# Rounded parts in the projections of the state-space stage: three one-pass products in place of one float32 product

## The reference, cut to what matters

```
[cq | ckv | kr | z | xBC | dt | mq | g] = x @ w_in
branch A: latent attention      (cq, ckv, kr)
branch B: xBC -> causal conv (4 taps) -> SiLU -> x, B, C in 4 groups
          dt = softplus(dt_raw + bias); decays exp(cum_i - cum_j)
          y  = ((C B^T) * decay * dt) x  +  C S exp(cum)  +  d_skip x
          S  = S exp(last) + (dt exp(last - cum) B)^T x      (also for the 8 sample states)
          y  = y * silu(z), RMS norm per group
branch M: cross-attention into 256 memory tokens
m  = sig(gA)(oA WoA) + sig(gB)(oB WoB) + sig(gM)(oM WoM);  x1 = LN(alpha x + m w_out)
y  = LN(alpha x1 + relu(x1 w_up + b_up)^2 w_down + b_down)
```

## Time and profile before

| | us |
|---|---|
| median of three runs | 1787.76 |
| the profiled execution | 1788.35 |
| its span, first to last instruction | 1786.7 |
| PE busy | 1712.9 (96%) |
| DVE, ACT, POOL busy | 734.7, 379.3, 370.1 |
| one group of the state-space stage (178.2 to 287.7) | 109.5 |

### The profile page before, as it was taken

One profiled execution on the slowest core, in us unless ns is written; L12 is line 12 of the kernel. 1 busy time (PEld: TensorE's weight loads), 2 busy tenths in 40 slices (PEclk: granted clock), 3 DMA queues, 4 the chain that ended last, 5 costly groups with the idle time before them and its releaser, 6 DMA issues.

```text
span 1786.7 us, 25145 instructions
## 1 busy us (share of the span) xinstructions
PE 1712.9 (96%) x10132; PEld 1416.8 (79%) x10132; DVE 734.7 (41%) x1284; ACT 379.3 (21%) x758; POOL 370.1 (21%) x330
## 2 busy tenths in 40 slices
PE   8999999999999999999899999999996999999995
PEld 6767667677777877787677777778895999999995
DVE  5565667665341121111222212311157871157345
ACT  2151332514312121111011111100124111111122
POOL 0040221402210000000233210000034433434332
PEclk9999999999999999999999999999999999999998
DMA  5324224252253222221777775432221222222221
GB/s 211 116 77 142 89 78 148 77 174 66 85 192 110 65 61 70 71 71 42 236 232 247 239 256 186 156 106 71 72 95 36 83 89 89 84 94 83 89 78 50
DMA packets 70405, 206.18 MB, mean 115 GB/s; under 512 B 10161, under 2 KB 26802, under 8 KB 65682
## 3 DMA queue, kind: packets, MB, share of 16 engines
q1 hardware_dynamic: 50384, 151.67, 26.3%
q10 hardware_dynamic: 13762, 31.93, 5.2%
q0 software_dynamic: 6144, 20.98, 4.0%
HBM read 189.68 MB, written 14.86 MB: 114 GB/s over the span
## 4 chain that ended last, share of the span: by engine, by line
PE 90%; DVE 5%; DMA 2%; ACT 1%; issue 1%; SPq 1%; POOL 0%; POOLq 0%; ACTq 0%; DVEq 0%
PE acc L1638 37%; PE acc L1678 23%; PE acc L1939 6%; PE acc L1905 3%; PE bank L1849 2%; PE acc L1887 2%; PE acc L2042 1%; PE bank L1954 1%; PE bank L1973 1%; PE bank L1955 1%; PE bank L1809 1%; PE bank L2056 1%; PE bank L1924 1%; PE bank L1930 1%; PE bank L2127 1%
## 5 line engine op out<-in xcount | busy, mean ns | idle before, releaser
L1638 PE MATMUL acc<-xt,ring 128*128 128x272 f32 x2496 | 602.4, 399 | 3.2 <-DMA ring<-in_stream 3.2
L1638 PEld LDWEIGHTS acc<-xt,ring 128*128 128x128 f32 x2496 | 472.9, 192 | 124.6 <-issue 30.0
L485 POOL TENSOR_TENSOR f_parts<-ring,f_parts 128x1024 fp32r<-128x1024 f32 x72 | 173.4, 2409 | 392.7 <-ACT f_parts L662 392.7
L1678 PE MATMUL acc<-x_parts,f_parts 128*128 128x272 f32 x1664 | 236.7, 292 | 16.8 <-DVE x_parts L1085 11.2
L1678 PEld LDWEIGHTS acc<-x_parts,f_parts 128*128 128x128 f32 x1664 | 221.2, 191 | 19.9 <-issue 13.3
L1678 PE MATMUL acc<-f_parts 128*128 128x272 f32 x1536 | 194.3, 289 | 0.0
L1678 PEld LDWEIGHTS acc<-f_parts 128*128 128x128 f32 x1536 | 193.6, 188 | 0.2
L463 POOL DMA_DIRECT2D work<-in_page_cols x128 | 68.8, 538 | 475.1 <-PE bank L1994 365.5
L662 ACT ACTIVATE f_parts<-ring 128x1024 fp32r<-128x1024 f32 x72 | 76.5, 1062 | 336.2 <-PE acc L1678 331.9
L1939 PE MATMUL acc<-branch,ring 128*128 128x272 f32 x512 | 120.0, 392 | 0.0
L1939 PEld LDWEIGHTS acc<-branch,ring 128*128 128x128 f32 x512 | 96.0, 190 | 18.8
(11 more groups left out here) (329 smaller groups left out, 1822.1 us busy)
## 6 DMA issues: line engine op xcount, KB each, us to landing
ring<-in_stream SPq DMA_DIRECT2D x216, 512.0 KB, 3.6
work<-in_page_cols POOLq DMA_DIRECT2D x128, 160.0 KB, 3.4
attended<-in_ssm_state ACTq DMA_DIRECT2D x8, 1024.0 KB, 6.2
work<-cum_rows SPq DMA_DIRECT2D x32, 256.0 KB, 4.5
out_ssm_s<-attended ACTq DMA_DIRECT2D x8, 1024.0 KB, 5.6
work<-in_ckv_rows ACTq DMA_DIRECT2D x64, 128.0 KB, 3.6
work<-in_ckv_rows SPq DMA_DIRECT2D x64, 128.0 KB, 3.0
work<-in_memk_cols SPq DMA_DIRECT2D x8, 1024.0 KB, 6.5
```

Of the source, the lines that this page charges most:

```text
L485: pool.tensor_tensor(split[j][1], ring[:, s * BLOCK:(s + 1) * BLOCK], split[j][0].bitcast(F), SUB).then_inc(sem["split_ready"], 1)
L1638: m = pe.matmul(acc[p][:, half, 0:width], w[:, k * P:(k + 1) * P], x(kk)[:, half * width:(half + 1) * width], start=kk == 0, stop=kk == n_ ...
L1678: m = pe.matmul(acc_half, w[:, k * P:(k + 1) * P], x[:, kk, of], start=kk == 0 and n == 0, stop=kk == last and n == 2)
```

## The change

Blocks 1 to 46 are treated as the later blocks are. x is split once into a rounded part XH, which takes the place of x, and a rest XL. For each block ACT makes the rounded weights w_hi (two buffers, `high_part`) and POOL the rest (`low_part`, into a second ring `ring_lo`). PE makes the products of w_hi with XH and XL for both halves first, then those of the rest with XH.

```diff
+            def high_part():
+                at = hi_at.next()
+                if at > SSM_SPLIT:
+                    return
+                s = at % RING
+                act.wait_ge(sem["blocks_begun"], CREDIT["blocks_begun"] + at)
+                act.wait_ge(sem[f"weights_in_slot{s}"], 16 * (loaded_before(at, s) + 1))
+                act.activation(w_hi[at % 2], ring[:, s * BLOCK:(s + 1) * BLOCK], ACT.Copy).then_inc(sem["hi_ready"], 1)
+                t.skip("hi_ready")
...
+            def low_part(n=1):
+                for _ in range(n):
...
+                    pool.wait_ge(sem["hi_ready"], t.next("hi_ready"))
+                    pool.tensor_tensor(ring_lo[:, slot], ring[:, slot], w_hi[at % 2].bitcast(F),
+                            SUB).then_inc(sem["split_ready"], 1)
...
+            def project_x(p, between=None):
+
+                at = used.value()
+                next_block()
+                wh, wl = w_hi[at % 2], ring_lo[:, at % RING * BLOCK:(at % RING + 1) * BLOCK]
+                pe.wait_ge(sem[f"acc{p}_free"], t.next(f"acc{p}_free"))
+                pe.wait_ge(sem["hi_ready"], t.next("hi_ready"))
+                for half, of in enumerate(halves):
+                    if half and between:
+                        between()
+                    for k in range(KC):
+                        if at == 1 and half == 0:
+                            pe.wait_ge(sem["x_split"], t.next("x_split"))
+                        for x in (XH, XL):
+                            m = pe.matmul(acc[p][:, half, 0:HT], wh[:, k * P:(k + 1) * P], x[:, k, of],
+                                          start=k == 0 and x is XH, stop=False)
...
+                pe.wait_ge(sem["split_ready"], t.next("split_ready"))
+                for half, of in enumerate(halves):
+                    for k in range(KC):
+                        m = pe.matmul(acc[p][:, half, 0:HT], wl[:, k * P:(k + 1) * P], XH[:, k, of], start=False,
+                                      stop=k == KC - 1)
+                m.then_inc(sem[f"acc{p}_ready"], 1)
```

To make room in memory several buffers now share one place: the tanh of a conv is written over the conv's input, so an evac waits for the finish of the conv two blocks earlier; the mask of B lies over the transposed B, so POOL's mask waits for the four state additions:

```diff
-        ext, cacc, th = ([k(EXT) for _ in range(2)] for _ in range(3))
+        ext, cacc = ([k(EXT) for _ in range(2)] for _ in range(2))
+        th = [work[:, j * EXT + 3:(j + 1) * EXT + 3] for j in range(2)]
...
             def evac(j):
+                n = evacuated.next()
+                if n > 2:
+                    act.wait_ge(sem["conv_ready"], n - 2)
                 act.wait_ge(sem[f"acc{j}_ready"], t.next(f"acc{j}_ready"))
...
                 pool.wait_ge(sem["b_tm_read"], t.next("b_tm_read"))
+                pool.wait_ge(sem["add_ready"], t.next("add_ready", NB))
```

The memory tokens are loaded behind the last read-out, and x (8 x 272 KB) again once PE has begun the first block of the memory keys:

```diff
-            load(blocks_before("sample") - blocks_before("mem_k"))
+            sp.wait_ge(sem["y_ready"], GC * GROUPS)
+            sp.dma_start(mem, mem_t).then_inc(sem["mem_loaded"], 16)
+            load(3)
+            sp.wait_ge(sem["blocks_begun"], CREDIT["blocks_begun"] + SSM_SPLIT + 2)
+            sp.dma_start(X, x_t).then_inc(sem["x0_loaded"], 16)
+            load(blocks_before("sample") - blocks_before("mem_k") - 3)
```

More of the change, by code:

```diff
@@ L248, in accv @@
             return acc[p][0:rows, :, 0:HT]
+        XH, XL = chunks(xt_hi, KC), chunks(ssm_parts, KC)
+        w_hi = [ssm_parts[:, KC * T + j * BLOCK:KC * T + (j + 1) * BLOCK] for j in range(2)]
         k = Carver()
-        ext, cacc, th = ([k(EXT) for _ in range(2)] for _ in range(3))
-        krope, a_rstd = k(T), k(T)
+        ext, cacc = ([k(EXT) for _ in range(2)] for _ in range(2))
+        th = [work[:, j * EXT + 3:(j + 1) * EXT + 3] for j in range(2)]
+        st_conv = k(NC * DEC_BATCH * 3).rearrange("p (c b t) -> p c b t", b=DEC_BATCH, t=3)
+        b_s = k(P, NS)
+        dec_p = k(NB * SSM_HEADS).rearrange("p (c h) -> p c h", h=SSM_HEADS)
+        k.at = 6 * T
+        off_s = k(GW)
+        c_mask = k(DEC_BATCH * NS).rearrange("p (b t) -> p b t", t=NS)
+        ecum_s = k(SSM_HEADS)
+        k.at = 6 * EXT
+        krope = k(T)
+        a_rstd = k(T)
         late_sq = [k(T) for _ in range(2)]
@@ L451, in _ @@
                 pool.tensor_tensor(sq_sum, zc[0], zc[2], ADD).then_inc(sem["sq_added"], 1)
+                low_part()
             pool.wait_ge(sem["state_and_ids_loaded"], 2 * 16)
@@ L624, in _ @@
             act.wait_ge(sem["acc1_free"], 1)
-            act.wait_ge(sem["vec_loaded"], 16)
-            act.wait_ge(sem["const_loaded"], 16)
+            hi_at = Count(None)
+            def high_part():
+                at = hi_at.next()
+                if at > SSM_SPLIT:
+                    return
+                s = at % RING
+                act.wait_ge(sem["blocks_begun"], CREDIT["blocks_begun"] + at)
+                act.wait_ge(sem[f"weights_in_slot{s}"], 16 * (loaded_before(at, s) + 1))
+                act.activation(w_hi[at % 2], ring[:, s * BLOCK:(s + 1) * BLOCK], ACT.Copy).then_inc(sem["hi_ready"], 1)
+                t.skip("hi_ready")
+            for c in range(KC):
+                if c % 2 == 0:
+                    act.wait_ge(sem[f"x{c // 2}_loaded"], 32)
+                act.activation(XL[:, c, :], X[:, c, :], ACT.Copy).then_inc(sem["rounded"], 1)
+            t.skip("rounded", KC)
+            high_part()
+            for c in range(KC):
+                act.wait_ge(sem["normed_even"], t.next("normed_even"))
+                if c < KC - 1:
+                    act.wait_ge(sem["dt_taken"], t.next("dt_taken"))
+                else:
+                    act.wait_ge(sem["acc0_ready"], 1)
+                act.activation(XH[:, c, :], X[:, c, :], ACT.Copy).then_inc(sem["x_split"], 1)
+            high_part()
+            act.wait_ge(sem["const_loaded"], 2 * 16)
             def root(a):
@@ L691, in latent @@
                 act.wait_ge(sem[f"acc{p}_free"], t.next(f"acc{p}_free"))
+                high_part()
+                if i == 3:
+                    act.wait_ge(sem["st_dec_ready"], DEC_BATCH * GROUPS)
                 act.activation(a_sq[i], dst, ACT.Square).then_inc(sem["squares_ready"], 1)
@@ L1088, in normalize @@
                             reciprocal(1)
+            for c in range(KC):
+                dve.wait_ge(sem["rounded"], t.next("rounded"))
+                dve.tensor_tensor(XL[:, c, :], X[:, c, :], XL[:, c, :].bitcast(F), SUB).then_inc(sem["normed_even"], 1)
             w = dtw
-            dve.wait_ge(sem["const_loaded"], 16)
+            dve.wait_ge(sem["const_loaded"], 2 * 16)
             dve.wait_ge(sem["acc0_ready"], t.next("acc0_ready"))
```

126 lines of the change are left out of this document (76 added, 50 removed).

## The result

The kernel after takes 1813.2 us (median of 4 runs, 1810.3 to 1818.5), the kernel before 1787.3 (4 runs): a ratio of 1.0146, 95% interval 1.0118 to 1.0174. I had forecast 1775 with a range of 1750 to 1800; the result lies outside it, 13 us above. The profiled execution took 1815.3 us.

A forecast was written before the change was run, and what follows sets the result against it. PE, busy 96% of the span, was taken as the bound. Head 0, three groups -6, last group -8 and reload +1 sum to -13 us: 1775 against the 1787.3 median, range 1750 to 1800.

The forecast's parts named there:

- Blocks: PE's blocks 1 to 46: 6.03 us instead of 7.40, saving 13.7 us a group and 63 in all as ceiling.
- Chunk additions and the pair in block 8: State additions of the chunks and in block 8: PE waits for DVE, 0.3 to 1.0 us more a group.
- Read-out 0: First read-out of a group: decays and scale_c come later, so PE waits 1.4 to 2.7 us.
- State additions: In block 7: PE arrives earlier than the chain from block 6's start; wait grows 2.0 to 9.2 us a group.
- Rival 1: Shared SBUF access decides at block 7's state additions: group +4, head +2, whole 1796 us; 0.33 together with rival 4.
- Transposes: Transposes of x behind the last evac and finish: PE waits 0 to 3.9 us more a group.
- Clock: Lower PE clock after waits: 0 to 1.7 us at read-out 0, up to 1.2 at the transposes.
- I take -2, the middle: Change of one conv group, taken between -10.0 and +6.0 us; three groups make -6.
- Head: Start to DVE's first read of a transpose: PE's savings against later dt work and convs, -4.4 to +4, taken 0.
- Last group: Group without conv behind it: nine blocks save 12.3 us, read-out 0 costs; -11 to -7, taken -8.
- Rival 3: Whole kernel comes out even: groups at about +1.7 us, 1788 us; chance 0.14.
- Rival 4: Blocks last 7 us instead of 6.03 because high parts or rests come late; near 1800 us, 0.33 together with rival 1.

The follow-up runs named there:

- e6: Kernel after with GpSimd's b_mask and its wait for the chunk additions moved behind the four scalings of C: 1812.4 us (1.012).
- e1: Kernel after with GpSimd's subtraction cut from 1024 columns to 8, the products with the rest reading the rounded weights instead: 1758.7 us (0.983).
- e3: Kernel after with GpSimd's subtraction made twice for each block, 46 more instructions: 1859.0 us (1.040).
- e12: e11 plus one useless GpSimd subtraction of 1024 columns for each float32 block up to block 33, nothing waiting for them: 1815.5 us (1.0149).
- e2: Kernel after with VectorE's two opening waits (constants, conv states) moved behind the eight subtractions of x: 1809.6 us (1.0118).
- e11: Kernel after with three products only in the last group's ten blocks, each block before that a float32 product as before: 1783.6 us (0.9976).

## Why the prediction was wrong, step by step

- *Blocks.* 6.0 us as forecast, 1.37 saved in each. At full clock, that is. PE's busy time in a group fell by 7.4 us and not by 13.7.
- *Chunk additions and the pair in block 8:* 0.3 to 1.0 more forecast, 0.2 measured (0.4 us as before and 0.2 at the pair). The meeting that was to cost here (5.32 us of L1358) came out at read-out 0.
- *Read-out 0:* 1.4 to 2.7 forecast, 3.0 measured. I had counted the decays and "turns with weigh", and not the chunk additions of DVE ahead of weigh. e6 shows that it didn't matter: without this wait the next is longer.
- *State additions:* 2.0 to 9.2 more forecast, 8.9 measured (11.0 against 2.1), with the chain at 21.3 us against my upper end of 21.6. Rival 1 was to decide from 19 us on, and it did. That the length fits the upper end so well is in part luck. Over the 14.4 us of the lower end the conv starts 2.0 us later, where I had 1.6 and 1.3; it takes 3.0 longer, where I had 3.8; and the finish takes 2.0 longer beside a subtraction, where I had 0.5 beside a scaling.
- *Transposes:* 0 to 3.9 more, 2.6 measured (4.3 and 0.7 against 2.4 us for all that PE waits at them).
- *Clock:* 0 to 1.7 and 1.2 forecast. Measured are about 6.3 us a group (13.7 saved by the blocks, 7.4 left in PE's busy time), at a granted clock of 0.89. Now three waits of a group are followed by a stretch at the lower level, and before it was the one in block 7. There I had written "the clock's price is paid there already", but the price grew with the wait: additions and half block together lose 3.0 us to it instead of 1.7. This is the one term of a group outside its own bounds by much, and why a group lies above my upper end.
- *The step that failed* is the value that I took between the ends: "I take -2, the middle", with the reason that "DVE is idle for a third of a group, so not every meeting costs". The rows that priced a meeting (4.51 against 2.60) spoke for the upper end, and that is where the meetings on DVE's chain came out: DVE's busy time grew by 20 us a group, and what PE waits for DVE at the three places from 4.5 us to 19.0. The measured group is +7.3. Idle time of an engine before PE's demand is no cover for a chain that PE waits for. e1, e3 and e12 show it in three ways. (The other half of the reason, that an instruction with an operand in PSUM passes, is right: see L1381 above.)
- *Head:* -4.4 to +4 forecast, +9.2 measured. The step that failed here is "put the dt work back by about 2 us": the first conv starts at 38.96 and not near 32.5 (before: 30.33). The cycle behind it was in its bounds, with 7.1 us a block. 3.6 of the delay is the wait for the constants, which I had not seen (e2): the diff joins the two loads in one semaphore, and DVE's opening wait now covers 1.1 MB, so the eight subtractions of x stand behind it. 4.7 is holds in the dt work, since e1, which has the same wait, starts its first conv at 34.27. In all the subtractions cost 12.8 us here: e1 has a head of 65.2.
- *Last group:* -8 forecast, -6.9 measured (block 2 to block 10's end, 84.8 us instead of 91.7). *Reload of x:* hidden; all that follows block 10 takes 1293.3 us instead of 1291.1, and the memory keys 27.9 as before.
- *Rivals.* Rival 1 came true, in its place and by its mechanism, but its price of +4 a group was 3 us too low, and that of +2 for the head 7. Rival 3 has a slip in its sum: groups at +1.7 give 1786, not 1788. Rival 4 fell: PE never waited for a rest of the weights.

## What to carry to other kernels

Before work is put on GpSimd, look not for its idle time but for what VectorE does then without an operand in PSUM: if that lies on a chain that TensorE waits for, the overlaps are added to it, 1 us here for each 1.8 to 2.7 of GpSimd (e1, e3, e12). The same subtraction on VectorE itself, 1.3 to 1.4 us behind the instructions that are waited for, was cheaper than 2.4 us on an engine that was busy for a quarter of a group. And when several terms of a sum have the same cause, they reach their upper ends together, so the middle of their sum isn't the likely value.

## What the runs showed of the hardware that I had not expected

- A VectorE instruction stays locked out over several GpSimd instructions that stand back to back: 5.32 us over three, 8.26 us over 19 (0.69 alone). The Trainium skill ("SBUF — State Buffer", "Who interferes with whom") has the pair held for the whole instruction, the loser blocked. These rows agree that it is blocked and not slowed, but the hold goes past the end of one instruction.
- The length of GpSimd's instruction does matter up to a point: cut in four, the same subtraction takes 3.6 us instead of 2.6 on GpSimd (184 pieces in 166.7 us, 46 blocks), and the kernel 17 us less. Cut in sixteen it takes 6.1, and the kernel gains nothing.
- Behind waits of 4.3, 3.0 and 11.0 us PE runs at the lower level (1.2 GHz instead of 2.4): the granted clock is 0.53 from 194.28 to 201.10, 0.54 from 227.78 to 230.84 and 0.55 from 262.56 to 269.70, and 1.00 from 269.70 to 277.00. Four products of a read-out take 0.43 us instead of 0.22, a half block 3.42 instead of 2.20. So waiting costs more than itself: 14.7 us more of idle time in a group went with about 6.3 us of slower work.
- "Busy" time of VectorE holds the time in which it is locked out: 72.1 us in the second group of e11 and 91.5 in that of e12, with the same 118 instructions.
